# Modulation and h of a hybrid SSM and attention layer in four quarters, and weight units of convolution and gate tiles in turn

## What is computed

```
shift, scale, gate = split(c @ w_ada + b_ada, 3)      # c: 1 x 1024, w_ada: 1024 x 3072
h = rmsnorm(x, g_pre) * (1 + scale) + shift           # 256 x 1024
z_ssm, xbc, dt, q, kv, nsa_gate, z_att, merge_gate = split(h @ w_in)
```

## Time and profile before

| | |
|---|---|
| median of 3 runs | 472.73 us (472.07 to 472.74) |
| the profiled execution, its own time | 470.02 us |
| its span, on which all times below stand | 468.2 us |
| mean granted clock of PE | 0.989 of 2.4 GHz |
| busy: PE, DVE, ACT, POOL | 438.0, 356.2, 259.1, 233.9 us |
| moved by DMA | 84.04 MB, mean 179 GB/s |

### The profile page before, as it was taken

One profiled execution on the slowest core, in us unless ns is written; L12 is line 12 of the kernel. 1 busy time (PEld: TensorE's weight loads), 2 busy tenths in 40 slices (PEclk: granted clock), 3 DMA queues, 4 the chain that ended last, 5 costly groups with the idle time before them and its releaser, 6 DMA issues.

```text
span 468.2 us, 9862 instructions
## 1 busy us (share of the span) xinstructions
PE 438.0 (94%) x3636; PEld 399.7 (85%) x3636; DVE 356.2 (76%) x617; ACT 259.1 (55%) x512; POOL 233.9 (50%) x236
## 2 busy tenths in 40 slices
PE   2689989999999989999899988999999999999995
PEld 2387989999999989987898987988998989999874
DVE  0466789999999999678799986688797767547733
ACT  3235885655564653456786936566475555534441
POOL 0154662368788689755363532245355362445440
PEclk9979999999999999999999999999999999999998
DMA  7999544564424444436449550735646444456102
GB/s 280 417 415 372 182 134 136 187 191 143 158 90 146 170 137 135 136 136 241 160 183 357 162 160 0 270 98 189 256 161 243 139 136 139 165 190 228 47 0 90
DMA packets 22391, 84.04 MB, mean 179 GB/s; under 512 B 2492, under 2 KB 2882, under 8 KB 21186
## 3 DMA queue, kind: packets, MB, share of 16 engines
q1 hardware_dynamic: 22344, 83.42, 50.5%
HBM read 82.36 MB, written 1.05 MB: 178 GB/s over the span
## 4 chain that ended last, share of the span: by engine, by line
PE 69%; DVE 8%; issue 7%; ACT 5%; POOL 4%; DMA 4%; SPq 1%; DVEq 0%; POOLq 0%; ACTq 0%
PE gemm L703 14%; PE gemm L705 14%; PE gemm L704 14%; DMA w_ada_shift_scale<-in_w_ada 3%; PE y_or_o L910 2%; DVE w_lo L1191 2%; PE gemm L679 2%; ACT w_hi L932 2%; PE y_or_o L791 1%; ACT probs L1149 1%; DVE conv_acc L1238 1%; POOL w_lo L1534 1%; PE score L874 1%; PE gemm L662 1%; PE small L584 1%
## 5 line engine op out<-in xcount | busy, mean ns | idle before, releaser
L1534 POOL TENSOR_TENSOR w_lo<-w_raw,w_hi 128x256 fp32r<-128x256 f32 (+1 forms) x117 | 135.4, 1162 | 178.9 <-ACT w_hi L932 144.2
L703 PE MATMUL gemm<-h_hi,w_hi 128*128 128x256 f32 x600 | 172.3, 287 | 4.5 <-DVE conv_acc L1238 2.0
L705 PE MATMUL gemm<-h_hi,w_lo 128*128 128x256 f32 x600 | 167.2, 279 | 0.0
L704 PE MATMUL gemm<-h_lo,w_hi 128*128 128x256 f32 x600 | 167.2, 279 | 0.0
L1191 DVE TENSOR_TENSOR w_lo<-w_raw,w_hi 128x768 fp32r<-128x768 f32 (+1 forms) x117 | 130.8, 1118 | 38.7 <-ACT w_hi L932 38.2
L932 ACT CAST w_hi<-w_raw 128x1024 fp32r<-128x1024 f32 x117 | 122.3, 1045 | 49.4 <-PE gemm L705 29.3
L703 PEld LDWEIGHTS gemm<-h_hi,w_hi 128*128 128x128 f32 x600 | 113.3, 189 | 8.3 <-issue 2.8
L704 PEld LDWEIGHTS gemm<-h_lo,w_hi 128*128 128x128 f32 x600 | 113.0, 188 | 0.7 <-issue 0.2
L705 PEld LDWEIGHTS gemm<-h_hi,w_lo 128*128 128x128 f32 x600 | 113.1, 188 | 0.0
L703 PE MATMUL gemm<-ynorm_hi,w_hi 128*128 128x256 f32 x128 | 36.4, 284 | 0.0
L705 PE MATMUL gemm<-ynorm_hi,w_lo 128*128 128x256 f32 x128 | 35.6, 278 | 0.0
(11 more groups left out here) (252 smaller groups left out, 895.0 us busy)
## 6 DMA issues: line engine op xcount, KB each, us to landing
w_raw<-in_wpack SPq DMA_DIRECT2D x133, 512.0 KB, 4.4
w_ada_shift_scale<-in_w_ada SPq DMA_DIRECT2D x8, 1024.0 KB, 15.8
x_T<-in_xT SPq DMA_DIRECT2D x2, 512.0 KB, 6.2
x_residual<-in_x_tok SPq DMA_DIRECT2D x1, 1024.0 KB, 4.8
out_tok_dram<-out_tok SPq DMA_DIRECT2D x4, 256.0 KB, 2.1
ada_gate_products<-in_gate_bias SPq DMA_DIRECT2D x1, 512.0 KB, 4.5
g_post_rows<-in_g_post_rows SPq DMA_DIRECT2D x1, 512.0 KB, 5.6
consts<-in_consts SPq DMA_DIRECT2D x1, 272.0 KB, 22.1
```

The lines of the kernel that those rows point to most:

```text
L703: nc.tensor.matmul(bank[:, 0:SEQ], w_hi, hi[:, k0 + k, :], start=first, stop=False)
L704: nc.tensor.matmul(bank[:, 0:SEQ], w_hi, lo[:, k0 + k, :], start=False, stop=False)
L705: last = nc.tensor.matmul(bank[:, 0:SEQ], w_lo, hi[:, k0 + k, :], start=False, stop=end)
L1534: nc.gpsimd.tensor_tensor(WL[:, n % LO_SLOTS, c:1024], RAW[:, u % RAW_SLOTS, c:1024], WH[:, n % HI_SLOTS, c:1024], ALU.subtract).then_inc( ...
```

## The change

Modulation and h go by quarters of the contraction (two of eight 128-row blocks each) in place of halves. w_ada is loaded as 16 parts of 512 KB, four for a quarter. The first ten units are re-cut into blocks ordered by quarter: 20 blocks (ten tiles, two k each) for each quarter, 2.5 units; all ten tiles are finished in units 7, 8 and 9. Quarters 0 and 1 are made on PE with N=128 in place of 256, quarter 1 in four pieces between blocks of quarter 0. Quarters 2 and 3 are made on DVE: eight linked passes over 128 x 512 (step `mod`), and PE then only sums over partitions with four products by a column of ones. `ada_columns(q+1)` stands before block 14 of the 20 of quarter q. The eight squares of x are added on DVE before one product with ones. Twelve products (KEEP_WARM) whose result nobody reads are put into the waits of the start. From unit 10 on, units of c and x alternate with units of z and za, and the hand-written places of the small steps move with them.

```diff
+FIRST_BLOCKS = [(tile, QUARTER_K * q + k) for q in range(QUARTERS) for tile in FIRST_TILES for k in range(QUARTER_K)]
+FIRST_READ = {7: (("dtg", 0), ("b", 0)), 8: (("b", 1), ("kc", 0), ("kc", 1), ("b", 2)),
+              9: (("b", 3), ("vc", 0), ("vc", 1), ("c", 0))}
+ADA_PIECES_AT, ADA_COLUMNS_AT = (4, 7, 9, 11), 14
+DVE_QUARTERS = (2, 3)
+KEEP_WARM = (6, 1, 3)
...
-    units = [("pair", i, half) for half in range(2) for i in range(len(PAIRS))]
-    units += [("c", j, 0) for j in range(1, 4)]
-    for g in range(SSM_GROUPS):
-        units += [("x", TPG * g + j, 0) for j in range(TPG)] + [("z", TPG * g + j, 0) for j in range(TPG)]
-    units += [("za", j, 0) for j in range(5)]
+    units = [("first", i, 0) for i in range(FIRST_UNITS)]
+    convs = [("c", j, 0) for j in range(1, 4)] + [("x", j, 0) for j in range(TPG * SSM_GROUPS)]
+    gates = [("z", j, 0) for j in range(TPG * SSM_GROUPS)] + [("za", j, 0) for j in range(5)]
+    for conv, gate in itertools.zip_longest(convs, gates):
+        units += [conv, gate] if conv else [gate]
...
-    put(len(PAIRS) - 2, ("ada2", 0))
-    put(6, ("dtT", 0))
-    put(7, ("dtA", 0), ("dtE", 0))
-    put(8, ("dtB", 0), ("dtL", 0))
-    put(10, ("dtC", 0))
+    put(0, ("ada", 1))
+    put(1, ("mod", 2))
+    put(2, ("ada", 2))
+    put(4, ("mod", 3))
+    put(5, ("ada", 3))
+    put(8, ("dtT", 0))
+    put(9, ("dtA", 0), ("dtE", 0))
+    put(10, ("dtB", 0), ("dtL", 0))
+    put(11, ("dtC", 0))
     put(13, ("acs", 0))
     for kind in range(3):
-        put(15 + kind, ("cb", kind))
+        put(18 + kind, ("cb", kind))
     for g in range(SSM_GROUPS):
-        b = 20 + 8 * g
+        b = 25 + 8 * g
...
-        put(b + 4, ("y", 2 * g), ("seg", 2 * g + 1))
-        put(b + 5, ("ea", 2 * g + 1))
...
+        put(b + 4 + last, ("y", 2 * g), ("seg", 2 * g + 1))
+        put(b + 5 + last, ("ea", 2 * g + 1))
+        put(b + 7 + 2 * last, ("y", 2 * g + 1))
...
-    put(58, ("ssq", 1))
+    put(64, ("ssq", 1))
     tiles = TPG * SSM_GROUPS
-    norm_units = [u for u in range(50, len(UNITS)) if UNITS[u][0] not in NATIVE or UNITS[u][2] % 2]
+    norm_units = [u for u in range(50, 62) if UNITS[u][0] not in NATIVE or UNITS[u][2] % 2]
+    norm_units = norm_units[:tiles // 2] + list(range(66, len(UNITS)))
...
-    put(at(("w1v", 0, 3)) + 1, ("kcp", 0))
+    put(at(("w1v", 0, 3)) + 3, ("kcp", 0))
```

SP's order of the start, the products on PE, and the sums on DVE:

```diff
+            weights_before = {3: (0,), 4: (1, 2), 8: (3, 4), 12: (5, 6)}
+            for n in range(QUARTERS * HALF_K):
+                q, k = n // HALF_K, 2 * (n % HALF_K)
+                for u in weights_before.get(n, ()):
                     sp.dma_start(RAW[:, u, :], wpack[u]).then_inc(w_in[u], 16)
-                sp.dma_start(ADA[:, s, k:k + 2, :], w_ada1[:, s, k:k + 2, :]).then_inc(ada_in[n], 16)
+                sp.dma_start(ADA[:, q, k:k + 2, :], w_ada1[:, q, k:k + 2, :]).then_inc(ada_in[n], 16)
...
+            def ada_columns(q):
+
+                if q in DVE_QUARTERS:
+                    pe.wait_ge(am_done, DVE_QUARTERS.index(q) + 1)
+                    for m in range(4):
+                        last = nc.tensor.matmul(ada_cols[:, m:m + 1], AM[:, P * m:P * m + P], cst("ones", 0, 1), start=True, stop=True)
+                    last.then_inc(modT_full, 1)
+                    return
...
+                        if q + 1 < QUARTERS:
+                            if at in ADA_PIECES_AT and q + 1 not in DVE_QUARTERS:
+                                ada_piece(q + 1, ADA_PIECES_AT.index(at))
+                            if at == ADA_COLUMNS_AT:
+                                ada_columns(q + 1)
...
+                elif what == "mod":
+                    for k in range(KT):
+                        if k % 2 == 0:
+                            dve.wait_ge(ada_in[HALF_K * i + k // 2], 16)
+                        if k == 0:
+                            ins = nc.vector.tensor_scalar(AM[:], ADA[:, i, k, :], par("c", k, k + 1), None, ALU.mult)
+                        else:
+                            ins = nc.vector.scalar_tensor_tensor(AM[:], ADA[:, i, k, :], par("c", k, k + 1), AM[:], ALU.mult, ALU.add)
+                        if k < KT - 1:
+                            link(ins)
+                    ins.then_inc(am_done, 1)
+                elif what == "ada":
+                    make_h(i)
```

More of the change, by code:

```diff
@@ L1 @@
+import itertools
 import numpy as np
@@ L246 @@
 RAW_SLOTS, HI_SLOTS, LO_SLOTS = 7, 4, 4
-H_POOL = (2, 6)
-H_DVE = tuple(k for k in range(KT) if k not in H_POOL)
-EARLY_SPLITS = range(len(PAIRS), 17)
+EARLY_SPLITS = range(HALF_K + 1, 17)
 OUT_K = 2
@@ L338, in build @@
     YT = place("y_tmp", [P, 2, SEQ], f32, at=over_at + 20 * kb)
-    SQS = place("y_sq_sums", [P, SSM_GROUPS, SEQ], f32, at=q_at + 28 * kb)
+    SQS = [place(f"y_sq_sums{n}", [P, 2, SEQ], f32, at=over_at + (22, 50)[n] * kb) for n in range(2)]
     RN = place("rstd_y", [P, SSM_GROUPS, SEQ], f32, at=q_at + 32 * kb)
@@ L396, in sem @@
         return sems[name]
-    ada_in = [sem(f"ada_in{k}") for k in range(KT)]
+    ada_in = [sem(f"ada_in{n}") for n in range(QUARTERS * HALF_K)]
+    sq_summed, am_done = sem("sq_summed"), sem("am_done")
     x_in = [sem(f"x_in{s}") for s in range(2)]
@@ L596, in _ @@
+            pe.wait_ge(cst_in_s, 16)
             pe.wait_ge(par_in_s, 16)
             pe.wait_ge(bank_zeroed, 1)
-            ada_rows(0)
+            keep_busy(KEEP_WARM[0])
+            for piece in range(HALF_K):
+                ada_piece(0, piece)
+                if piece == 1:
+                    pe.wait_ge(sq_summed, 1)
+                    nc.tensor.matmul(YB[:, 0:SEQ], cst("ones"), SQX[:, 0, :], start=True, stop=True).then_inc(ssx_full, 1)
+                if piece < HALF_K - 1:
+                    keep_busy(KEEP_WARM[1])
@@ L642, in weight_unit @@
                     return
-                if kind == "pair":
+                if kind == "first":
                     n = SPLIT_IDX[u]
@@ L646, in weight_unit @@
                     pe.wait_ge(lo_ready, n + 1)
-                    for kk in range(HALF_K):
-                        k = HALF_K * part + kk
-                        if j == 0:
+                    for c in range(8):
+                        q, at = divmod(8 * u + c, len(FIRST_BLOCKS) // QUARTERS)
+                        tile, k = FIRST_BLOCKS[8 * u + c]
+                        if tile == FIRST_TILES[0]:
                             pe.wait_ge(h_ready, k + 1)
-                        if u == len(PAIRS) - 1 and kk == 2:
-                            ada_columns(1)
-                        for m in range(2):
-                            c = 2 * kk + m
-                            if c == lo_share(n):
-                                pe.wait_ge(lo_rest_ready, n + 1)
-                            bank = home(PAIRS[j][m])
-                            w_hi = WH[:, n % HI_SLOTS, P * c:P * c + P]
-                            w_lo = WL[:, n % LO_SLOTS, P * c:P * c + P]
-                            first = k == 0 and PAIRS[j][m] not in SECOND_HALVES
-                            end = k == KT - 1 and PAIRS[j][m] not in FIRST_HALVES
-                            nc.tensor.matmul(bank, w_hi, HH[:, k, :], start=first, stop=False)
-                            nc.tensor.matmul(bank, w_hi, HL[:, k, :], start=False, stop=False)
-                            last = nc.tensor.matmul(bank, w_lo, HH[:, k, :], start=False, stop=end)
@@ L665, in weight_unit @@
+                        w_lo = WL[:, n % LO_SLOTS, P * c:P * c + P]
+                        first = k == 0 and tile not in SECOND_HALVES
+                        end = k == KT - 1 and tile not in FIRST_HALVES
+                        nc.tensor.matmul(bank, w_hi, HH[:, k, :], start=first, stop=False)
+                        nc.tensor.matmul(bank, w_hi, HL[:, k, :], start=False, stop=False)
+                        last = nc.tensor.matmul(bank, w_lo, HH[:, k, :], start=False, stop=end)
                     last.then_inc(unit_mm, 1)
@@ L1343, in _ @@
             scale_x(1)
-            for n in range(2, AHEAD):
-                split_lo(n)
+            split_lo(2)
+            for q in range(2, QUARTERS):
+                scale_x(q)
             done = ()
@@ L1714, in lay_out @@
             wpack[u] = ada[:, part, 2048:3072]
-        elif kind == "pair":
-            both = [tiles[k][n].reshape(P, KT, P)[:, HALF_K * part:HALF_K * (part + 1)] for k, n in PAIRS[j]]
-            wpack[u] = np.stack(both, 2).reshape(P, 1024)
+        elif kind == "first":
+            blocks = [tiles[tile[0]][tile[1]].reshape(P, KT, P)[:, k] for tile, k in FIRST_BLOCKS[8 * j:8 * j + 8]]
+            wpack[u] = np.concatenate(blocks, 1)
         elif kind == "out":
```

183 lines of the change are left out of this document (87 added, 96 removed).

## The result

The changed kernel takes 498.22 us (median of 4 runs, 497.14 to 498.80) against 472.40 us for the kernel before (4 runs, 471.20 to 472.74). The ratio is 1.0544, with a 95% interval of 1.0528 to 1.0559: 26 us slower. The forecast was 476.1 us with a range from 468 to 481. The direction was right, the size was not.

A forecast was written before the change was run, and what follows sets the result against it. PE's stream of products bounds the kernel, DVE second, DMA at the start. Terms +3.3 +2.0 +0.2 -1.3 -2.2 +1.4 = +3.4 give 473.4 us on the profiled execution, 476.1 on the median; range 468 to 481.

The forecast's parts named there:

- forecast A: Start: DVE's two sums, in series with PE through unit 8's split, set unit 10; 476.1 us, chance 0.42.
- The wait at z1: Unit 13: PE waits 3.8 us because c1's taps come late on DVE; +2.0 net, bounds -1.8 and +3.8.
- +3.3: Start up to unit 10: unit 10 begins at 62.4 us, 3.3 later than 59.10.
- blocks 34 to 39 at 0.22: Start, behind quarter 2's sums: 18 products at the fallen clock take 4.0 us, so unit 4 ends at 44.4.
- The second fall: Start, behind quarter 3's wait: PE's clock falls again, unit 10 at 64.2 (+5.1 in place of +3.3).
- +2.2: Behind unit 10: +2.0 for the wait at unit 13 and +0.2 for the later dt chain.
- -1.3: Units 17 to 49: PE's one wait there, 1.3 us for POOL, goes; bounds -1.3 and +1.5.
- -0.8: Units 50 to 76: -2.2 for moving kcp and ssq, +1.4 for norm work that comes later.
- of 5.2 us, some 3.8 find room between 228 and 250: Units 50 to 76: four norm tiles and a reciprocal mostly fit DVE's free time; +1.4, bounds 0 and +5.2.
- the -2.2 for moving kcp and ssq: Units 50 to 76: moving these steps takes away PE's waits of 1.5 and 0.7 us.
- D: Rival, DVE as bound: second clock fall (+1.8), moved norm work not absorbed (+3.8); +9.0, 481.7 us, chance 0.12.
- E: Rival, start: each DVE sum meets two POOL shares at 0.4, +0.8 twice; +5.0, 477.7 us, chance 0.05.

The follow-up runs named there:

- e_start_early: Kernel before with only the new start (quarters, two summed on DVE), each DVE sum placed one step earlier; 477.92 us, ratio 1.0102.
- e_start_warm: Kernel before with only the new start, plus 24 and 10 unread products ahead of PE's two waits for DVE's sums; 481.07 us, ratio 1.0175.
- e_order: Changed kernel with the old start (halves, pairs) put back and everything else as changed; 482.09 us, ratio 1.0233.
- e_norm: Changed kernel with the eight late norm tiles from unit 62 on and ssq 1 at 62; 489.84 us, ratio 1.0398.

## Why the prediction was wrong

**Right, and by its own steps.** PE's first product came at 19.72 (about 18.8). The fourteen passes with two operands take 0.75 us each, as the row that I took, and one sum takes 6.47 us (6.1). The sums are in series with PE through unit 8's split, as forecast A says: e_start_early and e_start_warm both show it. The wait at z1 is 3.8 us, the forecast one.

**The start: +10.1 in place of +3.3.** The chain was right, each link too short, and one link was left out.
- Unit 5's cast began at 33.41, not 31.2, and the first sum ended at 41.84, not 39.4: 2.4 us. The weights came 2.2 us later than by my count of bytes.
- The products by ones took 1.87 us each time, not 1.0: they run behind the wait, and at the lower clock (1.05 in e_start_early's first sum, at the full one). 0.9 twice.
- The step "blocks 34 to 39 at 0.22" held: unit 5 begins at 47.61, 3.2 us after the 44.4 of the text, of which 3.3 came in by the two points above.
- The second sum began 49.86 - 46.5 = 3.4 us late and its products ended at 58.26, not 53.6: 4.7 by then.
- I had let the clock stay full behind it, so that blocks 54 to 59 would be over before h was there. It fell: they are 18 products at 0.21 us, and quarter 3's first block came at 62.10, not 55.6. The second fall stood in the text as a bound of +1.8. It was the likely case: a wait of three us had been worked out there, and one of five had been charged with a fall.
- From that block to unit 10 it took 7.1 us (6.8). Together 69.20 - 62.4 = 6.8 us.

**Unit 10 to 14: +4.2 in place of +2.2.** The wait was right: 3.8 in place of 1.3, +2.5. What was missed is again the clock behind it: 13 products of unit 13 ran at 0.21 us, and with the small sums behind them the unit takes 5.16 us in place of 3.44, +1.7. The other 0.5 that I subtracted is 0.64 in the trace and stood at unit 17, outside this row.

**Units 14 to 61: +0.7 in place of -1.3.** Removing a wait for POOL was priced as a gain, and POOL's wait grew to 1.8. e_order shows that alternation gives PE nothing there.

**Units 61 to 77: +14.2 in place of -0.8.** This is the step that failed most. The text said that four norm tiles and a reciprocal, 5.2 us, fall into a stretch with 2.4 us free, "of 5.2 us, some 3.8 find room between 228 and 250", +1.4, upper bound +5.2. The bound took only DVE's busy time. e_norm gives 9.6 us back for the stretch. The norm work did not only add: its tiles stand ahead of the first head's maximum and exponentials in two in-order queues, PE waited 4.7 us there, and its clock fell to half behind that wait. The second fall, in unit 76, is no part of this, since e_norm has it too. And the -2.2 for moving kcp and ssq was wrong in sign, +2.75: of the two waits 1.5 grew to 2.1 and 0.7 fell to 0.2, and behind the 2.1 the clock fell, so that unit 62 takes 4.81 us in place of 3.19, +1.6 of the 2.75. The moved steps stand directly ahead of vcp, for which the queue of transfers stands, and I had named vcp nowhere. What that costs no run tells.

**The rivals.** D named the right engine and the right second fall of the clock, at +9.0, with a chance of 0.12; it is the nearest, at a third of the size. E's price for one meeting with POOL, 0.4 us, was right: a TENSOR_SCALAR pass takes 0.966 us beside a POOL split and 0.474 alone, a SCALAR_TENSOR_TENSOR 1.119 and 0.752. In the kernel after each sum met one POOL split in its first pass, not two. My reading of the earlier trace rows was not right: the split of 0.96 did not run alone, since a POOL split ran beside it from 29.90; it had begun 0.04 us before that one, and the split of 1.36 began 0.24 us after POOL's. The range failed because the bounds were worked out term by term, and all but one with PE's clock at full. The start twice, unit 13, unit 62 and unit 75 all hold the same thing, a wait of 2.1 to 5.6 us and a stretch at 1.2 GHz behind it, and the text priced it once.

## What to carry to other kernels

When a sum or a table load is put into an in-order queue, ask what stands directly ahead of it that is not yet needed: one place earlier gave back some 6 to 7 us here. Where the profile shows that PE's clock can fall behind a wait of a few us, add the half-speed stretch to the upper bound of every such wait, not to one of them, or put unread products ahead of it (3.5 us here). Do not take it as certain: of two waits of 3.6 us one had the fall and one had not. And price work that is moved into a nearly full stretch by what it stands in front of, not by the free time of its engine.
